# Eight edits to a one-core mixer and mixture-of-experts layer: convolution order, expert weight queues, and the last two experts

## The reference, cut to what matters

```python
proj = rms_norm(x) @ w_in                      # 1024 -> 3840
v = a_val * sigmoid(a_gate)                    # 768 channels
v = depthwise_conv(v, conv_w, width=31) + conv_b
...
x = x + (sigmoid(g_conv) * conv_out + sigmoid(g_ssm) * s5_out) @ w_out
h = rms_norm(x)
top_v, top_e = top_k(h @ w_router + b_router, 4);  gate = softmax(top_v)
# for each expert e, on the tokens that chose it:
gu = h @ w_gate_up[e] + b_gate_up[e]           # 1024 -> 2048, 8 MB of weights
g, lin = min(gu[:, :1024], 7), clip(gu[:, 1024:], -7, 7)
y = (g * sigmoid(1.702 * g) * (lin + 1)) @ w_down[e] + b_down[e]   # 4 MB of weights
x = rms_norm(x + sum over the four experts of gate * y)
```

## Time and profile before

| | us |
|---|---|
| timed runs, median (lowest, highest) | 1133.29 (1131.57, 1134.37) |
| the profiled execution's own time | 1130.38 |
| its span in the profile | 1128.6 |
| PE busy / DVE / ACT / POOL | 1078.7 / 283.3 / 176.7 / 75.2 |
| bytes moved by DMA | 432.17 MB, of which q1 (SP's queue) 431.64 |

### The profile page before, as it was taken

One profiled execution on the slowest core, in us unless ns is written; L12 is line 12 of the kernel. 1 busy time (PEld: TensorE's weight loads), 2 busy tenths in 40 slices (PEclk: granted clock), 3 DMA queues, 4 the chain that ended last, 5 costly groups with the idle time before them and its releaser, 6 DMA issues.

```text
span 1128.6 us, 14106 instructions
## 1 busy us (share of the span) xinstructions
PE 1078.7 (96%) x5857; PEld 483.1 (43%) x5858; DVE 283.3 (25%) x661; ACT 176.7 (16%) x303; POOL 75.2 (7%) x154
## 2 busy tenths in 40 slices
PE   7999899899999999999999999999999999999996
PEld 6888685533333333333333333333333333333332
DVE  3999661311111111111111111111111111111112
ACT  4011211311111111111111111111111111011112
POOL 3965100000000000000000000000000000000000
PEclk9999899999999999999999999999999999999999
DMA  8853379799999999999999999999999999999992
GB/s 228 271 170 129 146 312 383 288 376 419 415 428 434 429 431 430 433 433 432 429 432 434 430 432 432 433 431 432 431 434 430 432 430 434 432 432 430 431 419 111
DMA packets 41457, 432.17 MB, mean 383 GB/s; under 512 B 5471, under 2 KB 21261, under 8 KB 24428
## 3 DMA queue, kind: packets, MB, share of 16 engines
q1 hardware_dynamic: 41420, 431.64, 91.7%
HBM read 430.58 MB, written 1.05 MB: 382 GB/s over the span
## 4 chain that ended last, share of the span: by engine, by line
PE 80%; DVE 9%; DMA 5%; ACT 2%; issue 1%; another core or an unknown queue 1%; SPq 1%; DVEq 0%; POOL 0%; POOLq 0%; ACTq 0%
PE bank L1309 38%; PE bank L1321 19%; DVE bank L819 6%; PE bank L1267 5%; PE bank L1330 5%; DMA ring<-w_gate_up 4%; PE bank L1280 3%; PE bank L1232 2%; PE bank L1197 2%; ACT area L658 2%; PE bank L1301 1%; PE bank L1285 1%; PE bank L1089 1%; DMA ring<-w_in 1%
## 5 line engine op out<-in xcount | busy, mean ns | idle before, releaser
L1309 PE MATMUL bank<-ring,area 128*64 128x512 f32 x2048 | 450.4, 594 | 16.0 <-DMA ring<-w_gate_up 13.9
L1309 PEld LDWEIGHTS bank<-ring,area 128*64 128x64 f32 x2048 | 155.3, 137 | 292.7 <-issue 265.6
L1321 PE MATMUL bank<-ring,area 128*64 128x512 f32 x1024 | 226.8, 595 | 4.5 <-ACT area L658 2.4
L979 DVE TENSOR_SCALAR area<-bank 128x512 f32<-128x512 f32 x32 | 22.1, 692 | 745.3 <-PE bank L1309 745.3
L1321 PEld LDWEIGHTS bank<-ring,area 128*64 128x64 f32 x1024 | 71.7, 137 | 139.0 <-issue 132.4
L1089 PE MATMUL bank<-area,ring 128*128 128x256 f32 x480 | 106.6, 381 | 2.7 <-DMA ring<-w_in 1.5
L1089 PEld LDWEIGHTS bank<-area,ring 128*128 128x128 f32 x480 | 90.6, 191 | 17.5 <-DMA ring<-w_in 3.0
L664 ACT ACTIVATE area<-area 128x512 f32<-128x512 f32 x32 | 20.1, 629 | 464.9 <-DVE area L979 464.9
L819 DVE SCALAR_TENSOR_TENSOR bank<-ring,spread,bank 128x256 f32<-128x256 f32 x174 | 69.1, 484 | 0.0
L1267 PE MATMUL bank<-rows,pick 128*64 128x512 f32 x264 | 63.9, 605 | 0.4 <-DVE onehot L968 0.4
L1330 PE MATMUL bank<-area,spT 64*128 64x512 f32 x256 | 63.6, 615 | 0.7 <-ACT area L661 0.7
(11 more groups left out here) (236 smaller groups left out, 541.2 us busy)
## 6 DMA issues: line engine op xcount, KB each, us to landing
ring<-w_gate_up SPq DMA_DIRECT2D x52, 4096.0 KB, 38.5
ring<-w_down SPq DMA_DIRECT2D x27, 4096.0 KB, 34.7
ring<-w_gate_up SPq DMA_DIRECT2D x24, 1024.0 KB, 10.8
ring<-w_gate_up SPq DMA_DIRECT2D x12, 2048.0 KB, 14.5
ring<-w_in SPq DMA_DIRECT2D x15, 1024.0 KB, 9.6
ring<-w_down SPq DMA_DIRECT2D x14, 1024.0 KB, 17.5
ring<-w_down SPq DMA_DIRECT2D x3, 2048.0 KB, 9.8
ring<-w_out SPq DMA_DIRECT2D x1, 4096.0 KB, 14.3
```

The source lines that it names most:

```text
L1309: last = mm(bank[4 + b][64 * h:64 * h + 64, :], heT[:, k % 4, k // 4 * 64:k // 4 * 64 + 64], w[:, b * FF + h * 512:b * FF + h * 512 + 512] ...
L1321: last = mm(bank[6][64 * h:64 * h + 64, :], actT[:, k, :], w[:, k % 2, h * 512:h * 512 + 512], start=(k == 0), stop=(k == KD - 1))
```

## The change

1. **Convolution order.** Parts 0 and 1 of the projection are made in halves, the first channel block's gate and value before the second's (`half_bank`, `gated_half`), and w_in's second part is loaded directly behind the first, with the state-space inputs behind both. Taps go in two lanes of three blocks each, (0, 2, 4) and (1, 3, 5); the first lane starts alone with `LEAD = 10` taps, so the second is alone at the end. Eight taps stand in each scan step, the last included.
2. **ACT at the start.** The root's table is loaded before x arrives; the two sines come before the copy of the taps.
3. **Constants.** `ones` is written once at the start (it lies in `pick`), b_down in partitions 96 to 127 of the bias tile; PE's wait for POOL's last constants moves behind the convolution's sums.
4. **down_bias** moves from expert 0 to between expert 3 and the loop.
5. **w_down in the loop.** For experts 6 to 28 SP issues only the two w_gate_up DMAs. The one w_down DMA of 4096 KB is issued by ACT on a queue of its own, after ACT has copied expert e's result and passed its branch. SP still issues w_down of experts 2 to 5 and 29 to 31.
6. **Loads of the last experts.** Experts 29, 30 and 31 have parts `(4, 2, 2, 4)`, `(4, 2, 1, 1, 1, 1, 1, 1)` and `(2, 2, 2, 1, 1, 1, 1, 1, 1)`. SP issues w_gate_up of 30 and of 31 before w_down of 30 and of 31.
7. **Order of the last two experts.** PE makes expert 31's `gates_up` before expert 30's `down`, interleaves the two `down`s, and expert 31's gather of a next expert falls away.
8. **Final norm.** DVE multiplies by the gain while ACT squares; the scaling by the root's reciprocal is shared between DVE and ACT.

```diff
-SCAN_TAPS = 4
+SCAN_TAPS = 8
+LEAD = 10
-MIDDLE = 4, 4, 4
-LAST = 4, 2, 2, 1, 1, 1, 1
+MIDDLE = 4, 4
+END = {E - 3: (4, 2, 2, 4), E - 2: (4, 2, 1, 1, 1, 1, 1, 1), E - 1: (2, 2, 2, 1, 1, 1, 1, 1, 1)}
...
+        half_bank = [[bank[5][:, 0:T], bank[4][:, 0:T]], [bank[6][:, 0:T], bank[3][:, 0:T]]]
...
             load_win(0)
+            load_win(1)
             sp.dma_start(tap_rows, conv_w[0]).then_inc(tap_in, 16)
+            for ri, src in enumerate((ssm_b_re, ssm_b_im)):
+                sp.dma_start(ssb[:, ri, :, :], src[0].rearrange("(t g) p h -> (g p) t h", g=2)).then_inc(ssm_in, 16)
             for ri, src in enumerate((ssm_c_re, ssm_c_im)):
                 sp.dma_start(cld[:, ri, :, :], src[0].rearrange("(c g) h p -> (g h) c p", c=2)).then_inc(c_in, 16)
-            for ri, src in enumerate((ssm_b_re, ssm_b_im)):
...
-            load_win(1)
...
+            def refill_end(e, first, last):
+
+                j = 0
+                for n, signal in zip(END[e], end_in[e]):
+                    if first <= j < last:
+                        sp.wait_ge(chunk_used, (e - 2) * PER + j + n)
+                        load(e, j, e % 2, n, signal)
                     j += n
...
-            refill(E - 4, 0, MIDDLE)
-            refill(E - 3, 1, LAST, end_in)
-            sp.wait_ge(chunk_used, E * PER - PER)
+            refill(E - 6, 0, MIDDLE)
+            more_done(E - 5)
+            refill_end(E - 3, 0, PER)
+            more_done(E - 4)
+            refill_end(E - 2, 0, KD)
+            more_done(E - 3)
+            refill_end(E - 1, 0, KD)
+            refill_end(E - 2, KD, PER)
+            refill_end(E - 1, KD, PER)
+            sp.wait_ge(chunk_used, (E - 2) * PER + KD)
+            more_done(E - 2)
             sp.dma_start(at(0, D), norm_final_g.unsqueeze(0).to_broadcast([128, D])).then_inc(fin_in, 16)
...
+            act.wait_ge(consts, 1)
+            s.activation(neg_top, ident[:, 0:2], ACT.Sqrt)
...
-            act.wait_ge(params_pe, 2)
-            s.activation(taps[:, :, :], bank[7][:, 64:64 + KC * W].rearrange("p (k w) -> p k w", w=W), ACT.Copy)\
-                .then_inc(params_sb, 1)
             act.wait_ge(dve_th, 1)
             s.activation(mag, lrdt, ACT.Exp).then_inc(act_mag, 1)
             act.wait_ge(dve_rr, 1)
             s.activation(pw[:, 0, 1, :], rr, ACT.Sin).then_inc(act_sin, 1)
             s.activation(pw[:, 0, 0, :], ra, ACT.Sin).then_inc(act_sin, 1)
+            act.wait_ge(half_pe, 1)
+            s.activation(sig_a[:, 0, :], half_bank[0][0], ACT.Sigmoid).then_inc(half_sig, 1)
+            act.wait_ge(params_pe, 2)
+            s.activation(taps[:, :, :], bank[7][:, 64:64 + KC * W].rearrange("p (k w) -> p k w", w=W), ACT.Copy)\
+                .then_inc(params_sb, 1)
...
+            def expert(e, half, loads):
+
+                activate(e)
+                copy_next(e)
+                act.wait_ge(chunk_used, e * PER + PER)
+                y_row_copy().then_inc(y_row, 1)
+                more_blocks(e)
+                if loads:
+                    act.dma_start(grid(at(half * PER + KD, 4 * CH), KD, D), dn_v[e + 2]).then_inc(quad_in[half * 3 + 2], 16)
...
+            with act.Fori(len(EARLY) // 2, E // 2 - 3) as i:
                 for half in range(2):
+                    expert(i * 2 + half, half, True)
+            expert(E - 6, 0, True)
...
+            lanes = [[(k, w) for k in range(half, KC, 2) for w in range(W)] for half in range(2)]
+            order = lanes[0][:LEAD]
+            for n in range(KC // 2 * W):
+                order += lanes[0][LEAD + n:LEAD + n + 1] + lanes[1][n:n + 1]
...
+            gated_half(0)
             dve.wait_ge(params_sb, 2)
-            taps_of(0, range(W))
-            gated(1)
-            taps_of(1, range(W))
-            gated(2)
+            scanning = len(order) - SCAN_TAPS * ST
+            taps_of(order[:scanning])
...
-                taps_of(2, range(SCAN_TAPS * t, SCAN_TAPS * (t + 1) if t < ST - 1 else W))
+                taps_of(order[scanning + SCAN_TAPS * t:scanning + SCAN_TAPS * (t + 1)])
...
-            project(0)
+            project(0, (0,))
+            project(1, (0,))
             pe.wait_ge(tap_in, 16)
...
-            project(1)
+            project(0, (1,))
+            project(1, (1,))
...
-            pe.wait_ge(down_in, 32)
-            for n in range(4):
-                down_bias(n)
             fetch_next(0)
...
+            pe.wait_ge(down_in, 32)
+            for n in range(4):
+                down_bias(n)
+            with pe.Fori(len(EARLY) // 2, E // 2 - 2) as i:
                 for half in range(2):
                     expert(i * 2 + half, half, [i * 16 + n for n in later[half]])
-            for half in range(2):
-                expert(E - 2 + half, half, LAST if half else [(E // 2 - 1) * 16 + n for n in later[half]])
+            expert(E - 4, 0, [(E // 2 - 2) * 16 + n for n in later[0]])
+            expert(E - 3, 1, E - 3)
+
+            gates_up(E - 2, 0, E - 2)
+            add_last(E - 2)
+            fetch_next(E - 2)
+            turn_act(E - 2)
+            turn_next(E - 2)
+            pe.wait_ge(a_T, E - 1)
+            gates_up(E - 1, 1, E - 1)
+            down(0, E - 2, range(4))
+            turn_act(E - 1)
+            down(0, E - 2, range(4, KD))
+            pe.wait_ge(a_T, E)
+            down(1, E - 1, range(4), act_2, 7)
+            pe.wait_ge(y_row, E - 1)
+            scatter(spT_2, yrow_2)
+            down(1, E - 1, range(4, KD), act_2, 7)
+            more_blocks(E - 2, 0, E)
+            more_blocks(E - 1, 1, E)
             pe.wait_ge(y_row, E)
```

More of the change, by code:

```diff
@@ L207, in build @@
         quad_in = [sem(f"quad_in{i}") for i in range(SLOTS // 4)]
-        end_in = [sem(f"end_in{i}") for i in range(len(LAST))]
+        end_in = {e: [sem(f"end{e}_in{i}") for i in range(len(parts))] for e, parts in END.items()}
         stored = sem("stored")
@@ L718, in _, with activate, copy_next @@
-            s.activation(neg_top, ident[:, 0:2], ACT.Sqrt)
+            def activate(e):
+                act.wait_ge(g_clip, e + 1)
+                sigmoid().then_inc(g_sig, 1)
+            def copy_next(e, act_dst=actT, spread_dst=spT):
+                act.wait_ge(h_pe, e + 2)
+                h_row_copy().then_inc(h_row, 1)
+                act.wait_ge(aT_pe, e + 1)
+                a_T_copy(act_dst).then_inc(a_T, 1)
+                act.wait_ge(hT_pe, e + 2)
+                h_T_copy().then_inc(h_T, 1)
+                act.wait_ge(spT_pe, e + 1)
+                spread_copy(spread_dst).then_inc(spT_sb, 1)
@@ new lines, in expert @@
+            def expert(e, half, loads):
[6 more added lines that the diff above has]
+                    act.dma_start(grid(at(half * PER + KD, 4 * CH), KD, D), dn_v[e + 2]).then_inc(quad_in[half * 3 + 2], 16)
+            with act.Fori(0, len(EARLY) // 2) as i:
+                for half in range(2):
+                    expert(i * 2 + half, half, False)
@@ new lines, in _ @@
+            with act.Fori(len(EARLY) // 2, E // 2 - 3) as i:
+                for half in range(2):
+                    expert(i * 2 + half, half, True)
+            expert(E - 6, 0, True)
+            for e in range(E - 5, E - 2):
+                expert(e, e % 2, False)
+            activate(E - 2)
+            copy_next(E - 2, spread_dst=spT_2)
+            activate(E - 1)
+            root_table()
+            act.wait_ge(spT_pe, E)
+            spread_copy().then_inc(spT_sb, 1)
+            act.wait_ge(aT_pe, E)
@@ new lines, in _, with taps_of @@
+            lanes = [[(k, w) for k in range(half, KC, 2) for w in range(W)] for half in range(2)]
+            order = lanes[0][:LEAD]
+            for n in range(KC // 2 * W):
+                order += lanes[0][LEAD + n:LEAD + n + 1] + lanes[1][n:n + 1]
+            def taps_of(some):
+                for k, w in some:
+                    if w == 0 and k in (1, 2, 4):
+                        if k == 1:
+                            gated_half(1)
+                        else:
+                            gated(k // 2)
+                    if (k, w) == (0, W - 1):
+                        dve.wait_ge(raw_ready, 1)
+                    tap(k, w)
@@ L1042, in _ @@
[L1042 to L1047 removed]
+                    gate_and_lin(e)
+                    more_blocks(e, half)
+            pick_next(E - 2, 0)
+            dve.wait_ge(chunk_used, (E - 2) * PER + KD)
+            gate_and_lin(E - 2)
+            dve.wait_ge(chunk_used, (E - 2) * PER + 2 * KD)
@@ L1065, in _ @@
                 pe.wait_ge(diag_ready, t + 1)
-                last = mm(bank[6][:, t * 128:t * 128 + 128], ones_1, diag[:, t, :], start=True, stop=True)
+                last = mm(bank[6][:, t * 128:t * 128 + 128], ones, diag[:, t, :], start=True, stop=True)
             last.then_inc(spread_pe, 1)
@@ L1288, in arrived @@
             def arrived(half, j, uses):
-                if uses is LAST:
-                    starts = [sum(LAST[:p]) for p in range(len(LAST))]
```

(10 more changed lines are left out.)

333 lines of the change are left out of this document (193 added, 140 removed).

## The result

The changed kernel takes 1138.32 us (median of 20 runs, 1132.56 to 1145.12), the kernel before 1131.01 (20 runs beside them, 1128.54 to 1134.37). The ratio is 1.0059, with a 95% interval of 1.0047 to 1.0072: slower by 0.6%, where 1.5% faster was forecast. The profiled execution took 1141.08 us, its span 1139.2; it is one of the slower of the 20, 2.8 above their median.

What follows compares the result with a forecast made beforehand. The weight stream was taken to set the end. Terms -5.2 - 2.8 - 0.6 + 1.2 - 9.4 - 0.7 = -17.5 took the profiled 1130.38 to 1112.9 us, or 1115.8 against the median, told as 1116; range 1109 to 1125.

Steps and rivals of the forecast that it cites:

- The mixer: Before expert 0: an earlier convolution start gives -5.2 us, and PE's clock kept up behind it -2.8.
- Rival C: At the start: early loads don't land in time, 5.2 and half the clock's gain are lost; 1122 us, chance 0.12.
- `down_bias`: Moved behind expert 3: closes the stream's small early hole, -0.6 us, bounds 0 and -3.6; 3.6 cost without cover.
- The ACT queue: Loop's w_down loads on ACT instead of SP: counted 0; at a rate of 415 GB/s it would cost +29 us.
- rival D: In the loop: ACT's w_down takes bandwidth from w_gate_up needed first, up to 9.7 us once; 1126 us, chance 0.06.
- Rival E: Experts 6 to 28: two interleaved queues lower the stream's rate; at 415 GB/s +29 us, 1145 us; chance 0.05.
- F: As a rival: two queues fill small gaps between DMAs and run above 433 GB/s; 1112 or 1113 us, chance 0.07.
- Behind the last byte: New order of the last experts: PE ends 2.4 us behind the last landing instead of 11.8, so -9.4.
- rival B: PE's pause at 123 still drops the clock, or last experts meet a fetch pause; 1119 to 1120 us, chance 0.20.
- the bad bound is one more fetch pause: Behind the last byte: a pause of 1.94 us and its slow clock, 1.9, leave a gain of only -5.6.
- Finer pieces: Last experts' loads: more single-slot and two-slot loads at a lower rate cost +1.2 us, bounds 0 and +3.
- Norm: Final norm: earlier table load, gain multiplied beside the squares, last scaling split; -0.7 us, bounds 0 and -1.5.

Runs made afterwards that it cites:

- experiment 1: The changed kernel with only down_bias put back into expert 0, between its gates_up and its gather; 1134.07 us, ratio to the kernel before 1.0023.
- both edits undone: The changed kernel with down_bias back in expert 0 and w_down of the loop back on SP; 1123.85 us, ratio to the kernel before 0.9924.
- experiment 5: The kernel with both edits undone, but w_down of experts 18 to 28 issued by ACT; 1135.67 us, ratio to the kernel before 1.0038.
- experiment 6: The kernel with both edits undone, with experts 28 and 29 back in the loops and 29 loaded as 4, 4, 4; 1124.24 us, ratio 0.9937.
- the kernel without the bodies: The kernel of experiment 6 without the two skipped more_blocks bodies on PE ahead of the final scatter; 1120.42 us, ratio 0.9918.
- experiments 6 and 7: The latter: the kernel of experiment 6 with the old order and loads of the last two experts, mixer and norm new; 1126.28 us, ratio 0.9954.
- the second kernel of heading 1 and 2: The changed kernel with only w_down of the loop back on SP, down_bias staying moved; 1126.73 us, ratio to the kernel before 0.994.

## Why the prediction was wrong, step by step

The sum was to be 1112.9 for the profiled execution and came to 1141.08, 28.2 more. By the medians it is 22.5 (1138.32 against 1115.8): the forecast started from an execution 2.9 below its median and was met by one 2.8 above. The rows split the 28.2 but for 0.1 outside the span: the last landing F at 1108.9 instead of 1099.1 (+9.8); PE's end at F + 19.0 instead of F + 2.4 (+16.6); and 11.3 from there to the end of the span instead of 9.6 (+1.7).

**The mixer: right.** The first half gate came at 19.61 (19.1 in the text, 19 to 20 as told), the second at 25.76 (24.9), the convolution ended at 124.22 (123.7), and L1317 took 2.86 at full clock (2.7). Together 7.35 by L1317's end (8.0 forecast). 1.3 of it was lost on the way to expert 0, to a gather that took 3.33 instead of 1.94 at 206.42; in experiment 1 it took 1.94 and expert 0 started at 210.94, so this belongs to the execution. With both edits undone 5.8 reached expert 27, in the later kernels less. Rival C is refuted: the early loads came in time.

**`down_bias`: the step that failed first.** "Later the 3.63 are covered by PE's lead." At that place the loads wait for PE to free slots (SP issues the next w_gate_up at 341.77), not PE for the loads, so PE has no lead. Ahead of the loop PE pauses for instructions anyway (1.65), and the 8 matmuls behind took 6.37 at clock 0.50, not 3.63; expert 4's matmuls took 15.87. Slots came free so late that the DMA engines ran empty near 339. In expert 0, where it had stood, it had been cover itself: without it PE waits 1.93 for DVE's activation, and `down` takes 7.69 instead of 7.09. Gate and up of expert 0 to expert 1 take 30.1 us, as against 30.4 before. The bill is 4.4 us at expert 27, and 4.9 at the last landing (1107.0 against 1102.0), where -0.6 was counted, with "without cover they would cost 3.6" as the bound. Undone alone, it gives back some 4 us (ratio 1.0059 to 1.0023), and beside SP's single queue some 2 to 3 (0.994 to 0.9924, intervals that overlap).

**The ACT queue: the step that failed most.** It was counted at 0, and rival D got a chance of 0.06, because "experts 29 to 31 come in one queue". The mechanism of D was told right, and its reach and its price (up to 9.7) too small. The two queues share the engines, so w_down, of which the ACT queue holds one load at a time, lands 23.4 after its issue, and w_gate_up, which PE needs first, 44.8. At expert 27 the weights are 14.3 late, which at 432 GB/s is 6.2 MB, one and a half w_down loads delivered too early. To be repaid, that needs a tail in which PE is faster than the stream by as much. From expert 28 on PE's own pace gains at most 1.8 an expert, and pauses of 2.33 and 1.90 with 15.62 us behind each took that away. So the disorder did reach the end: 12 us of experiment 5, from the last eleven experts, and nothing to be seen from the first ten (16 and 17 were in neither). That "only the place of PE's waits moves" holds for those first ten alone.
Rival E is refuted by 432 GB/s at full share in 500 to 600, and so is F. The forecast's slower side lay on the wrong mechanism: rate, not order.

**Behind the last byte: mis-sized, apart from the disorder.** With the queue in order PE ends at F + 5.5 (1107.50 against 1102.0), not F + 2.4. The missing 3.1 are the two pauses, 1.78 and 1.76, that rival B spoke of: without them PE ends at F + 2.9 (experiment 6) and at F + 3.4 in the kernel without the bodies. So "the bad bound is one more fetch pause" was too few, and no term had the pause at the end. The 19.0 of the kernel after are then the 2.4 of the forecast, these 3.1, 10.7 for the queue (experiment 1 ends at 1119.33, 16.2 behind its landing at 1103.1), and 2.8 more in the kernel after, whose two pauses are 2.33 and 1.90 with 15.62 us behind each, where experiment 1 has 1.62 twice with 13.93. Whether the low clock comes there is in part a matter of the execution: of the 20 timed runs of the kernel after, the slowest two have a mean granted clock of 0.987 and 0.986 and the profiled one 0.988, the five fastest 0.992 to 0.996. The order itself does what it was meant to: 6.0 us between experiments 6 and 7, with the pause at the end set aside.

**Finer pieces: about right.** 1.2 was forecast; from 1095 to 1100 the rate is 419, and in the earlier trace rows 415. From expert 27's mark to the last landing it is 128.13 with both edits undone and 126.76 before, so 1.4 longer. No run had the pieces alone.

**Norm: no gain.** From the last `down` to the end of the span it is 10.4 in the kernel without the bodies, 10.5 in the one with the old end, and 10.3 before. The forecast of -0.7 is refuted; in the kernel after it is 11.3, as the steps over the two bodies stand in it. In the kernel without the bodies the first square starts 1.18 behind the scatter's start (1.37 before), and from the second root's start to the scaled output it is 1.23 (1.84 before). But from the first square to the second root it takes 4.34 instead of 3.87, and from the scaled output to the end of the span 2.9 instead of 2.6, which eats the gain. Which edit does this was not tried.

What stays open: why the low clock followed some pauses and not others (below), why the pause at the two bodies is 4.50 in one kernel and under 2 in six, and how much of the mixer's 7.35 the two parts gave, as they were never run apart.

## What to carry to other kernels

A second queue changes what arrives first even when the total rate stays the same. Where one stream is the bound, keep the order in which the consumer needs the bytes, above all over the last experts, as here nothing behind them could repay what came early.
Work moved out of a stage is free only where the new place has a lead, and the old place did not use it as cover; look in both for who waits next. Then look at the jumps: bodies that are never entered can still cost when they are stepped over with nothing beside them, from 0.9 to 3.8 us beyond the 0.70 for ACT's copy here, and one test around both took some 4 us off the kernel where it was most.

## What was unexpected in the hardware

- Pauses of PE for its own instructions stand where written-out code or a loop begins: 1.62 to 2.44 before the last experts in most kernels, 1.65 to 2.97 ahead of the loop. At the two skipped bodies PE stood 1.61 to 1.99 in six kernels and 4.50 in one.
- The length of the pause doesn't tell whether the clock falls. Behind 1.90 and 2.33 the 64 matmuls took 15.62; behind 1.94 once 15.62 and once 13.93 (experiment 5); behind 1.76 and 1.78, and behind 2.08 and 2.17 in the second kernel of heading 1 and 2, 13.93. Ahead of the loop, a pause of 1.65 with `down_bias` behind it ended in clock 0.50, and one of 1.83 with the gate and up matmuls behind it (experiment 1) did not.
- Two queues with large loads moved 432 GB/s between them, as one did, with landings of 23.4 and 44.8 us.
- SP's issues of the last eight w_down parts took up to 4.25 us each in the kernel after (median 3.05), and up to 9.57 with both edits undone, where each took 0.33 before. The pieces landed 2.5 apart all the same, so no cost is seen.
